# Memory cross-attention: the reciprocal ahead of the probabilities' low half, and three convolution steps spread over an iteration

## The reference

```
def memory_cross_attention(zq, mem, ...):
    mk, mv = keys (normed) and values of the 256 memory tokens
    q = rms_norm(zq.reshape(B, S, 4, 128), xq_norm_w)
    s = einsum("bshd,bmhd->bhsm", q, mk) * 128 ** -0.5
    p = softmax(s, axis=-1)
    o = einsum("bhsm,bmhd->bshd", p, mv)
```

## Time and profile before

| | |
|---|---|
| median of three runs | 1972.78 us |
| profiled execution | 1971.36 us, span 1969.6 us |
| busy share of the span: PE, DVE, ACT, POOL | 97%, 56%, 37%, 5% |
| mean granted clock of TensorE | 0.995 |
| cross stage | first score matmul at 695.5 us, first value product of the last tile at 802.2 us |
| first value product of the first branch stage | 826.7 us |

### The profile page before, as it was taken

How to read it: one execution, slowest core, us unless ns; L and a number is a source line. 1 busy time by engine, 2 the same in 40 slices (tenths; PEclk the granted TensorE clock), 3 DMA queues, 4 the chain that set the end, 5 groups by cost and what they waited for, 6 DMA issues and landing times. The chain is left out here.

```text
span 1969.6 us, 24174 instructions
## 1 busy us (share of the span) xinstructions
PE 1918.9 (97%) x9113; PEld 1646.5 (84%) x9113; DVE 1098.5 (56%) x1413; ACT 738.2 (37%) x1324; POOL 99.1 (5%) x153
## 2 busy tenths in 40 slices
PE   6999999999999998999999999989999999999999
PEld 5788999999998887787888887868888888878887
DVE  5535632453351776897425625478778787643433
ACT  6323532442243154312613322445544454432222
POOL 1101110111010010000100001000000000000000
PEclk9999999999999999999999999999999999999999
DMA  7211221021113101102113405113232232264312
GB/s 245 97 43 44 71 70 43 12 81 49 43 60 113 43 1 43 43 22 65 43 33 93 154 23 171 65 43 97 64 96 74 86 93 67 85 239 146 111 48 75
DMA packets 112412, 152.33 MB, mean 77 GB/s; under 512 B 13705, under 2 KB 60809, under 8 KB 112329
## 3 DMA queue, kind: packets, MB, share of 16 engines
q1 hardware_dynamic: 104265, 140.60, 22.0%
q10 hardware_dynamic: 8064, 10.59, 1.5%
HBM read 122.73 MB, written 28.43 MB: 77 GB/s over the span
## 5 line engine op out<-in xcount | busy, mean ns | idle before, releaser
L240 PE MATMUL psum<-whi,act_lo 128*128 128x512 f32 x768 | 314.9, 410 | 3.5 <-DVE act_lo L1431 2.9
L242 PE MATMUL psum<-whi,act_hi 128*128 128x512 f32 x768 | 304.4, 396 | 0.0
L241 PE MATMUL psum<-wlo,act_hi 128*128 128x512 f32 x768 | 304.4, 396 | 0.0
L240 PEld LDWEIGHTS psum<-whi,act_lo 128*128 128x128 f32 x768 | 194.9, 254 | 18.7 <-issue 4.5
L242 PEld LDWEIGHTS psum<-whi,act_hi 128*128 128x128 f32 x768 | 195.1, 254 | 15.3
L241 PEld LDWEIGHTS psum<-wlo,act_hi 128*128 128x128 f32 x768 | 196.0, 255 | 13.2
L240 PE MATMUL psum<-act_hi,wlo 128*128 128x512 f32 x512 | 202.2, 395 | 1.3 <-DVE wlo L198 1.3
L242 PE MATMUL psum<-act_hi,whi 128*128 128x512 f32 x512 | 199.6, 390 | 0.0
L241 PE MATMUL psum<-act_lo,whi 128*128 128x512 f32 x512 | 199.3, 389 | 0.0
L193 ACT CAST whi<-stage 128x512 fp32r<-128x512 f32 x200 | 120.3, 621 | 180.9 <-PE psum L242 172.6
L198 DVE TENSOR_TENSOR wlo<-stage,whi 128x512 fp32r<-128x512 f32 x200 | 129.0, 686 | 94.7 <-ACT whi L193 93.9
(11 more groups left out here) (248 smaller groups left out, 3572.5 us busy)
## 6 DMA issues: line engine op xcount, KB each, us to landing
stage<-in_w_in SPq DMA_DIRECT2D x144, 256.0 KB, 4.0
u_raw<-in_w_up SPq DMA_DIRECT2D x44, 512.0 KB, 5.0
gated_scratch<-g_buf SPq DMA_DIRECT2D x22, 512.0 KB, 2.7
gated<-gated_scratch SPq DMA_DIRECT2D x22, 512.0 KB, 3.5
d_stage<-in_w_down SPq DMA_DIRECT2D x44, 256.0 KB, 2.8
group_out<-ob ACTq DMA_DIRECT2D x24, 256.0 KB, 2.1
grp<-group_out SPq DMA_DIRECT2D x24, 256.0 KB, 3.2
stage<-in_w_mem_kv SPq DMA_DIRECT2D x16, 256.0 KB, 8.5
```

Of the source, the lines that this page charges most:

```text
L240: nc.tensor.matmul(dst, lhs[1], rhs[0], start=first, stop=False, skip_group_check=True)
L241: nc.tensor.matmul(dst, lhs[0], rhs[1], start=False, stop=False, skip_group_check=True)
L242: return nc.tensor.matmul(dst, lhs[0], rhs[0], start=False, stop=last, skip_group_check=True)
```

## The change

In `tiles_dve` the reciprocal of the sums of tile i-2 moves from behind the low half of the probabilities of tile i-3 to ahead of it. `free_time()` is called three times in an iteration and not once: behind the scaling of the queries, behind the low half of the probabilities, and at the end, as before. In the cross stage each call issues one step of the convolution and not three. The number of steps in an iteration and their order stay.

```diff
                 tl = tile_of(part, i, "KQX")
                 if tl:
                     norm_dve_scale(dve, tl.n, tl.index, tl.qn)
+                free_time()
+                tl = tile_of(part, i - 2, "X")
+                if tl:
+                    dve.wait_ge(p_done, tl.a + 1)
+                    nc.vector.reciprocal(recip_l[:, tl.a % 2, :], softstat[:, tl.a % 4, 0, :]).then_inc(l_recip, 1)
                 tl = tile_of(part, i - 3, "QX")
                 if tl:
                     c = NH * tl.width
                     dve.wait_ge(pt_hi_done, tl.a + 1)
                     nc.vector.tensor_tensor(tl.pt[1][:, 0:c], banks(5)[:, 0:c], tl.pt[0][:, 0:c].bitcast(F32),
                                             ALU.subtract).then_inc(pt_lo_done, 1)
-                tl = tile_of(part, i - 2, "X")
-                if tl:
-                    dve.wait_ge(p_done, tl.a + 1)
-                    nc.vector.reciprocal(recip_l[:, tl.a % 2, :], softstat[:, tl.a % 4, 0, :]).then_inc(l_recip, 1)
+                free_time()
                 tl = tile_of(part, i - 4, "X")
...
             def vector(dve):
-                tiles_dve(dve, CROSS_TILES, lambda: conv(dve, 3))
+                tiles_dve(dve, CROSS_TILES, lambda: conv(dve, 1))
```

## The result

The changed kernel takes 1954.25 us (median of four runs, 1952.27 to 1954.80) where the kernel before takes 1972.67 beside it: a ratio of 0.9904, 95% interval 0.9887 to 0.9921. The profiled execution took 1954.80 us, 16.56 less than that of before; the sum had said 16.9 less.

The account below looks back on a forecast made before the run. A DVE-ACT loop of 13.12 us against PE's 10.89 was taken to hold the cross stage. 17.5 less 0.6 gave 16.9 us saved: 1954.5 us for the profiled execution, 1955.9 for the median; range 1954.6 to 1961.0.

Parts of the forecast that it names:

- the sum: Cross stage: 17.5 us earlier last-tile values less 0.6 us of waiting left, 16.9 us saved.
- The loop through DVE and ACT holds the stage: Cross stage: a loop through DVE and ACT alone sets 13.12 us per iteration, against PE's own 10.89.
- The times of one new iteration: Cross iteration from its maximum M: reciprocal M+3.2, scaling M+4.0, output's low half M+6.45, next maximum possible at M+9.5.
- PE loses 2.2 us in each full iteration: Cross stage before the change: PE's work takes 10.89 us of a 13.12 us iteration, so it loses 2.2.
- PE sets the pace at 10.89: Cross stage after the change: DVE's loop of 9.5 us is below PE's 10.89, so PE sets the pace.
- One wait is left, 0.6 us: Last tile's iteration: PE waits for the output's low half, 4.3 us of slack against 4.9 us of splits.
- A step beside ACT costs what it does alone: Cross stage: a convolution step beside ACT's exponentials and scalings takes 1.19 us; upper bound 3.5 us by POOL's ratio.
- The wait of 2.1 us behind the stage stays: Middle of the first branch stage: PE's 2.1 us wait for split weights stays, hanging on 35 steps after a product.
- The halved clock: Cross stage, around 755 to 766 us: clock 0.50 follows waits and goes with them; otherwise about 2.5 us longer.
- the account of the 17.5 us: Last tile's values, 802.20 to 784.7 us: 12.2 of printed waits, some 0.16 more per wait, and the halved clock.
- The page on contention: Skill rule to improve the busiest engine first; since the change touches only DVE, it would forecast no change.
- 1.4 less than the median of 1972.78: Last step: profiled execution before, 1971.36 us, lies 1.4 under the median, so 1954.5 becomes 1955.9 for the median.

Follow-up runs that it names:

- another change: Two convolution steps moved from the middle of the first branch stage (32 to 30) to its start (14 to 16), against the changed kernel: 1951.35 us beside 1955.07.
- all three steps at one place: Changed kernel with its reciprocal order kept, but all three convolution steps ahead of the output's low half: 1971.24 us, ratio 0.9995 to the kernel before.
- the spreading alone: Changed kernel with the reciprocal put back behind the probabilities' low half, the three steps still spread: 1961.28 us, ratio 0.9939 to the kernel before.
- the reordering alone: Changed kernel with the reciprocal still moved ahead, but the three convolution steps together at the iteration's end: 1962.26 us, ratio 0.9945 to the kernel before.

## Why the prediction was right or wrong

- *The loop through DVE and ACT holds the stage:* right. Undoing either half brings back the waits that this reading gives it, in place and in size: 97.8 us for 97.5 forecast, 93.15 for 93.0.
- *The times of one new iteration:* right to 0.1 us at each point that was named.
- *"PE loses 2.2 us in each full iteration":* wrong. That is the loop's time less PE's own, 13.12 - 10.89. PE's query transposes in the earlier trace rows are 12.40 and 10.89 us apart, so PE lost 1.5 us in one full iteration and nothing in the next. The sum did not use this figure, since it goes from PE's chain to the last tile's values.
- *PE sets the pace at 10.89:* right, 10.88. PE's chain without waits, 784.7 us, plus 0.6 is 785.3; measured 785.68, in a trace whose stage began 0.37 later than before.
- *One wait is left, 0.6 us:* right in kind and place, 0.44 in size.
- *A step beside ACT costs what it does alone:* right, 1.27 to 1.28 us. The upper bound of 3.5 us, taken from POOL, described nothing of DVE.
- *The wait of 2.1 us behind the stage stays:* right; it took another change to remove it.
- *The halved clock:* the account of the 17.5 us nearly adds up (12.2 of waits, 0.16 for each of 13 waits and 2.5 of slow matmuls make 16.8), but the clock has no fixed price. The clock did stay at 1.00 in the changed kernel's stage. But the stage before is no longer with 17 us at half clock than with 6.8, because PE's waits shrink by what the matmuls grow. In a stage that PE paces, all three steps at one place point the other way: there the missing clock did cost. So "about 2.5 us longer if the halving stayed" is neither shown nor refuted, since no trace of the changed kernel has a halved clock in this stage. The Trainium skill, page "TensorE: Matmul & The Clock Gate", section "What's actually happening", says that idleness lets the clock fall and activity lifts it. The traces agree in part: below 1.00 in all eight of before, 1.00 in all three after, but 1.00 also in the two runs of one half each, where PE still waited 5.9 and 2.9 us in the stage.
- *The page on contention:* the Trainium skill's "Perfetto Trace Analysis", section "Identifying the Most-Contended Engine", says to improve first the engine with the highest occupancy. No gain from work on DVE at 56% was the prediction's reading of it, and that reading fell: the gain is 0.96% from the order on that engine alone, and it is time in which PE, the engine at 97%, no longer waits.

The step that failed is the last one, from the sum to the median and the range. From one profiled execution to the next the sum of 16.9 us held: 16.56 was measured. The prediction then added "1.4 less than the median of 1972.78" to the changed kernel as a constant. That term measured -0.55: the changed kernel's profiled execution took 1954.80 us and its median is 1954.25. This is 2.0 us too much, more than the 1.65 by which the forecast was too high. A likely reason is the place near 1200 us, where the profile of before had full clock and that of the changed kernel lost 2.9 us. The range could not take this up, since its lower end is "1955.3 less 0.7 for scatter", and the 0.7 came from the three runs shown of before, 1972.56 to 1973.24. Over all runs the kernel before spreads from 1968.71 to 1974.61 and the changed one from 1951.70 to 1956.63, 5.9 and 4.9 us. The 0.35 us by which the range was missed are small beside that: the two other medians of the changed kernel, 1955.07 and 1955.33, lie inside the range.

The medians differ by 18.4, 17.4 and 17.8 us in the three comparisons. That they all lie above 16.9 is not explained. Over the traced executions alone the means are 1971.7 (eight) and 1955.1 us (three), 16.5 apart, and they have the time ahead of and behind the cross stage nearly alike; whether the untraced ones of before lose a little more at half clock outside it was not settled.

## What to carry to other kernels

When PE is 97% busy and still waits a little in many iterations, write down the loop that starts and ends at the same instruction, with the start of each member, and ask which filler work lies in it at a time when nobody else can run; moved into the gaps where that engine already waits, it is free up to the pace of the next engine, and no further. The iterations at the ends of a pipeline, and those with extra work, have less room than the full ones, so fit the filler to them. A range needs the scatter of many executions, not of three, and one profiled execution does not lie at a fixed distance from the median.

## What the runs showed of the hardware that was not expected

TensorE's granted clock fell to 0.50 in the cross stage behind waits of PE of 2.9 us and less. With all three steps at one place, one wait of 2.03 us (up to 727.07 us) was enough, the only one in the stage until then. Yet the waits alone do not decide it. With the spreading alone PE waited 2.24 us (up to 759.86 us), with the reordering alone 1.3, 1.4, 0.8 and 0.8 us between 751 and 764 us, and the clock stayed at 1.00. At 1199 us two executions of the kernel before have the same wait of 2.09 us, and one has the half clock behind it and the other has not.

What a halved clock costs depends on who holds the stage. Where other engines hold it, 17 us at half clock made the stage no longer than 6.8 us (106.7 us with either; no execution had none). Where PE is nearly the bound it came on top: 7.0 us of waits and 8.5 us of missing full speed made the stage 15.4 us longer. So a small wait in a stage that PE sets can cost more than its printed length.
